# Loading w_up in pairs of ring slots by half-partition transfers, in a one-core decoder block with a mixture of experts

## The reference

```
def expert_block(args):
    xb, e = args
    u = xb @ w_up[e] + b_up[e]
    glu = jnp.minimum(u[:, :D_FF], SWIGLU_LIMIT)
    lin = jnp.clip(u[:, D_FF:], -SWIGLU_LIMIT, SWIGLU_LIMIT)
    act = glu * jax.nn.sigmoid(SWIGLU_ALPHA * glu) * (lin + 1.0)
    return act @ w_down[e] + b_down[e]
```

## Time and profile before

| | |
|---|---|
| median of 3 runs | 1800.74 us |
| profiled execution, its own time | 1798.54 us |
| its span, first to last instruction | 1796.7 us |
| mean granted TensorE clock | 0.965 of full speed |
| TensorE matmul busy | 1632.7 us (91%) |
| VectorE, ScalarE, GpSimd busy | 533.8, 283.1, 211.4 us |
| read from HBM, written | 456.89 MB, 18.87 MB |
| loads of `w_up` | 256 transfers of 1 MB |
| loads of `w_down` | 128 transfers of 1 MB |

### The profile page before, as it was taken

How to read it: one execution, slowest core, us unless ns; L and a number is a source line. 1 busy time by engine, 2 the same in 40 slices (tenths; PEclk the granted TensorE clock), 3 DMA queues, 4 the chain that set the end, 5 groups by cost and what they waited for, 6 DMA issues and landing times.

```text
span 1796.7 us, 31195 instructions
## 1 busy us (share of the span) xinstructions
PE 1632.7 (91%) x12187; PEld 743.7 (41%) x12188; DVE 533.8 (30%) x1388; ACT 283.1 (16%) x561; POOL 211.4 (12%) x202
## 2 busy tenths in 40 slices
PE   3995979978999758999999999999999999999992
PEld 2442437543454313444434434444443443444441
DVE  2012464221031243223224223323322422322331
ACT  3013324211130201001101101100100110110113
POOL 1000000051000110111121121121111112112111
PEclk9998989989999879999999999999999999999996
DMA  6121111223100557999999999999999999999993
GB/s 213 47 94 47 47 47 48 94 77 105 47 1 0 228 185 309 367 380 387 379 355 401 382 364 390 385 369 384 381 376 381 377 394 364 389 389 369 390 360 107
DMA packets 105522, 467.49 MB, mean 260 GB/s; under 512 B 14062, under 2 KB 14114, under 8 KB 72624
## 3 DMA queue, kind: packets, MB, share of 16 engines
q1 hardware_dynamic: 89152, 438.33, 62.2%
q0 software_dynamic: 13744, 25.46, 5.9%
q10 hardware_dynamic: 2592, 3.25, 0.5%
HBM read 456.89 MB, written 18.87 MB: 265 GB/s over the span
## 4 chain that ended last, share of the span: by engine, by line
PE 86%; DVE 6%; ACT 4%; issue 2%; ACTq 1%; DMA 1%; POOL 0%; DVEq 0%; POOLq 0%
PE bank L835 37%; PE bank L613 20%; PE bank L863 12%; PE bank L872 6%; PE bank L824 1%; PE bank L803 1%; PE bank L813 1%; PE bank L755 1%; DVE arena L1269 1%; PE bank L630 1%; PE bank L805 1%; PE bank L816 1%; ACT L945 1%; PE bank L850 1%; ACT L946 1%
## 5 line engine op out<-in xcount | busy, mean ns | idle before, releaser
L835 PE MATMUL bank<-ring,arena 128*32 128x512 f32 x6144 | 679.2, 594 | 0.0
L835 PEld LDWEIGHTS bank<-ring,arena 128*32 128x32 f32 x6144 | 227.7, 110 | 402.6 <-issue 335.5
L863 PE MATMUL bank<-ring,arena 128*32 128x512 f32 x2048 | 267.8, 592 | 0.0
L613 PE MATMUL bank<-ring,actT 128*128 128x512 f32 x576 | 252.0, 597 | 1.9 <-DVEq L355 1.9
L1450 DVE TENSOR_SCALAR actT<-bank 64x512 f32<-64x512 f32 x64 | 43.7, 683 | 435.1 <-PE bank L835 434.1
L613 PEld LDWEIGHTS bank<-ring,actT 128*128 128x128 f32 x576 | 109.3, 192 | 137.7 <-issue 134.5
L872 PE MATMUL bank<-ring,arena 128*32 128x512 f32 x1024 | 157.9, 592 | 0.0
L863 PEld LDWEIGHTS bank<-ring,arena 128*32 128x32 f32 x2048 | 112.8, 110 | 96.2
L530 POOL DMA_INDIRECT arena<-h_rows,arena x33 | 35.1, 1062 | 901.3 <-DVE arena L1434 901.3
L1097 ACT ACTIVATE actT<-actT 128x512 f32<-128x512 f32 x32 | 20.2, 630 | 526.2 <-DVE actT L1450 526.2
L613 PE MATMUL bank<-actT,ring 128*128 128x512 f32 x192 | 82.8, 593 | 1.2 <-DVEq L355 1.2
(11 more groups left out here) (284 smaller groups left out, 1308.8 us busy)
## 6 DMA issues: line engine op xcount, KB each, us to landing
ring<-in_w_up SPq DMA_DIRECT2D x256, 1024.0 KB, 6.5
ring<-in_w_down SPq DMA_DIRECT2D x128, 1024.0 KB, 7.8
ring<-in_w_in SPq DMA_DIRECT2D x12, 1024.0 KB, 8.2
ring<-in_w_ck SPq DMA_DIRECT2D x4, 1024.0 KB, 5.6
ring<-in_w_cv SPq DMA_DIRECT2D x4, 1024.0 KB, 6.2
ring<-in_w_out SPq DMA_DIRECT2D x4, 1024.0 KB, 5.7
ring<-in_w_cq SPq DMA_DIRECT2D x4, 1024.0 KB, 6.1
ring<-in_w_co SPq DMA_DIRECT2D x4, 1024.0 KB, 6.3
```

The costliest lines, as they stand in the source:

```text
L613: mm = pe.matmul(o, lhsT, rhs, start=(k == 0), stop=(k == KT - 1))
L835: mm = pe.matmul(bank[g][32 * t:32 * t + 32, :], lhsT, w[:, 512 * t:512 * t + 512], start=False, stop=(k == KT - 1))
L863: mm = pe.matmul(bank[3][r:r + 32, :], hTA[:, k % 4, g, k // 4, :], w[:, 512 * t:512 * t + 512], start=False, stop=(k == KT - 1))
```

## The change

A pair of `w_up` chunks (256 rows) is now laid over a pair of neighbouring ring slots. Row 256j + 2p + u goes to partition p, slot u, so partition p holds two rows that lie together in HBM, 16 KB. The pair is loaded by two transfers of 1 MB: one fills the partitions 0 to 63 of both slots, the other the partitions 64 to 127. So each transfer is 64 partitions of 16 KB where it was 128 of 8 KB. Both are issued when both slots are free, and TensorE waits for both before the first matmul of the pair. `rows_T` reads every second column of the gathered rows, so that partition p of the operand for slot u is feature 256j + 2p + u. `w_down` is loaded as before.

```
+        xgA_u, xgB_u = [t_.rearrange("p (c n u) -> p c n u", n=P, u=2) for t_ in (xgA, xgB)]
...
         def up_chunk(e, c):
-            return A["w_up"][0][e, P * c:P * c + P, :]
+            half = 64 * (c % 2)
+            return A["w_up"][0].rearrange("e (c p u) n -> e c p (u n)", p=P, u=2)[e, c // 2, half:half + 64, :]
...
             def load_up(q, o, e):
-                for c in range(UP_CHUNKS):
-                    sp_.wait_ge(chunk_used, q * PER_EXPERT + (o + c + 1))
+                for c in range(0, UP_CHUNKS, 2):
+                    sp_.wait_ge(chunk_used, q * PER_EXPERT + (o + c + 2))
                     slot = (o + c) % RING
-                    sp_.dma_start(ring_flat[:, slot, :], up_chunk(e, c)).then_inc(chunk_in[slot], 16)
+                    pair = ring_flat[:, slot:slot + 2, :].rearrange("p s n -> p (s n)")
+                    for u in range(2):
+                        sp_.dma_start(pair[64 * u:64 * u + 64, :], up_chunk(e, c + u)).then_inc(chunk_in[slot + u], 16)
...
-                    pe.transpose(bank[5][:, P * i:P * i + P], xgA[:, P * i:P * i + P], ident[:, :])
+                    pe.transpose(bank[5][:, P * i:P * i + P], xgA_u[:, i // 2, :, i % 2], ident[:, :])
...
-                    t = pe.transpose(bank[6][:, 64 * i:64 * i + 64], xgB[0:64, P * i:P * i + P], ident[0:64, 0:64])
+                    t = pe.transpose(bank[6][:, 64 * i:64 * i + 64], xgB_u[0:64, i // 2, :, i % 2], ident[0:64, 0:64])
...
             def up_pair(q, o, pair):
+                expert_chunk_in(pe, q, o + 2 * pair)
+                expert_chunk_in(pe, q, o + 2 * pair + 1)
                 for k in (2 * pair, 2 * pair + 1):
-                    expert_chunk_in(pe, q, o + k)
```

## The result

| | before | after |
|---|---|---|
| median | 1799.76 us (4 runs, 1798.44 to 1803.96) | 2380.43 us (4 runs, 2378.89 to 2384.82) |
| profiled execution | 1798.54 us | 2381.77 us |
| its span | 1796.7 us | 2380.0 us |
| mean granted TensorE clock | 0.965 | 0.891 |

The ratio is 1.3225 (95% interval 1.32 to 1.325): slower by 580.7 us. Forecast were 2335 us, between 2050 and 2450. One more run of the kernel before moved its median from 1800.74 to 1799.76 us. Ratios compare fast executions alone (within 1.5% of a kernel's fastest), so where executions scatter a ratio does not follow from the medians.

A forecast was written before the change was run, and what follows sets the result against it. TensorE bounds the kernel at 34.46 us a pass; DMA work becomes 38.7 + 10.6 + 2.4 = 51.7 us, 17.2 more, so 31 passes add 534 us to 1798.5: 2332.5, stated as 2335 us, range 2050 to 2450.

The forecast's parts named there:

- The bound before: Expert passes before the change: TensorE sets the pace at 34.46 us a pass, against 34.1 us of DMA work.
- They come in time narrowly: Weights in the expert passes: their queue and GpSimd's keep the engines busy 98%, so slightly slower transfers become the bound.
- Half the partitions: `w_up` transfers: 64 partitions run like 32, at 217 GB/s; `w_up` takes 38.7 us a pass instead of 21.1.
- The rest of the DMA work: Other transfers of a pass, taken as unchanged: `w_down` 10.6 us, gathers and scatters 2.4 us.
- Pieces of 16 KB: Longer pieces in `w_up` transfers: taken as zero, bounded by 0.1 us a pass on either side.
- The ring and SyncE: `w_up` slots and issue: waiting for two slots and both halves costs nothing with a full queue; SyncE's fewer waits, zero.
- rival 3: `w_up` ring: full transfer rate, but pairs issued too late; at most +124 us, 1925 us; chance 0.05.
- The transposes: Strided reads for `rows_T`: taken as zero under the waiting, bounds no gain to 1.1 us a pass.
- That the halves don't compete: `w_up` transfers: both halves flow at once at 397 GB/s; 1801 us, or up to 1836; chance 0.12.
- rival 2: `w_up` transfers: halves overlap in part, 284 GB/s, a pass of 42.5 us, 2051 us; chance 0.05.
- its rival: TensorE's clock falls around its waits; at most some 3 us a pass, 2430 us; chance inside the forecast's 0.78.
- the signs that I named: Changed profile: some 250 GB/s, passes of 51.7 us, waits about 4.5 us before most pairs, landing near 20 us.

## Why the prediction was right, and where it was off

**The bound before.** TensorE, in passes of 34.46 us: right, and less work on TensorE shortened the kernel. "They come in time narrowly" was right in kind; the room was 2.2 us a pass, since a full DMA share is not the same as no room.

**Half the partitions.** The step that carries the sum. Right: transfers to the lower or upper 64 are as slow as the bias loads to 32 partitions, and the second half doesn't help the first. The reason given beside it was not right: "what differs is how few partitions are the target". The even and the odd 64 are as few and run at the full rate; it is that each target lies in one half. From the count alone, treating 64 like 32 was a choice, and it came out right because these 64 are one half. The size was slightly off: I took 217 GB/s, the mean of 213 and 220, and measured are 212. `w_up` takes 32 x 1.239 = 39.6 us of an engine in a pass, not 38.7. The longer window of the earlier trace rows had it, and the shorter one, at a share of 1.04, led away from it.

**The rest of the DMA work** was taken over unchanged as 13.0 us. It became 53.3 - 39.6 = 13.7: GpSimd's transfers, 5.3% of 53.3, are 2.8 us instead of 2.4, and `w_down` with 172 ns for each of its 64 packets an engine 11.0 instead of 10.6. Together the two terms are the 1.6 us by which a pass was forecast too short, 50 us in all; the forecast was 45 under the result.

**Pieces of 16 KB** were put at zero within 0.1 us. On all partitions that is right (665 ns against 2 x 333). On halves the kernel with pieces of 8 KB is 54 us shorter, of which the packets of `w_up` explain 1.2 us a pass; the prediction had nothing for that.

**The ring and SyncE**: zero, confirmed by the kernel that fills slot by slot; with it rival 3 falls. **The transposes**: zero here, under cover, and 0.32 us a pass without it, within my bounds of 0 and 1.1.

**The rivals.** That the halves don't compete is refuted. The part overlap of rival 2, 284 GB/s, didn't show. The clock fell as its rival said, to half in a part of every pass (0.73 in the mean from 1300 to 1306 us, 0.88 from 1506 to 1515), and cost nothing. Of the signs that I named, 250 GB/s was 245, passes of 51.7 us were 53.3, the landing of near 20 us was 17.5 in the median; waits of 4.5 us were 3.1 in the mean (382.4 / 122), shorter because TensorE worked longer at the lower clock: 53.3 - 382.4 / 31 = 41 us of a pass where it was 34.5.

## What to carry to other kernels

Look at which partitions a transfer reaches, not at how many or at how long its pieces are: 0 to 63 or 64 to 127 alone had half of the rate here, while the even partitions, 32 to 95, or all had all of it. Where a buffer has to be loaded in two parts, split it by columns or take every second partition. And a DMA share near 1 doesn't tell what the engines could do: take work from the engine that bounds the kernel and see how far the time follows.

## What was not expected

A strided read slows the weight load of a float32 transpose: 209 ns instead of 140 for 128 partitions, 216 instead of 138 for 64, at a step of two elements. The price of halves is not linear in their number: passes of 34.9, 40.5, some 44 to 46 and 53.3 us with none, one, two and four pairs by halves. And on halves a piece of 16 KB took a little more than two of 8 KB, 1239 ns against 2 x 599; whether its length is the reason isn't shown.
